# Modulation weights stored by output column and reduced along rows, with the first stage cut into nine groups

## The reference, cut to what matters

```python
c_act = jax.nn.silu(c)                                   # (1, 2048)
mod = c_act @ w_ada[l] + b_ada[l]                        # (2048, 12288): 100 MB
sh_a, sc_a, gt_a, sh_f, sc_f, gt_f = split(mod, 6)
h = _rmsnorm(x, norm_mix[l]) * (1.0 + sc_a) + sh_a
p = h @ w_in[l]                                          # (2048, 9296)
... attention (c_q, c_kv, k_pe) and gated delta rule (q, k, v, z, b, a) from p ...
mix = (g_a * y_a + g_b * y_b) @ w_o[l]
x = x + gt_a * mix
h = _rmsnorm(x, norm_ffn[l]) * (1.0 + sc_f) + sh_f
gate, up = split(h @ w_gate_up[l], 2)
x = x + gt_f * ((silu(gate) * up) @ w_down[l])
... final norm, then the second block: a_w_in_2, w_s, a_w_out_2 ...
```

## Time and profile before

| | us |
|---|---|
| median of 3 runs | 2282.92 (2281.2 to 2283.67) |
| the profiled execution | 2283.3 |
| its span | 2282.0 |
| TensorE busy in it | 2227.7 (98%) |
| VectorE | 1514.7 (66%) |
| ScalarE | 1017.8 (45%) |
| DMA, mean rate | 223 GB/s, 507.8 MB |

### The profile page before, as it was taken

How to read it: one execution, slowest core, us unless ns; L and a number is a source line. 1 busy time by engine, 2 the same in 40 slices (tenths; PEclk the granted TensorE clock), 3 DMA queues, 4 the chain that set the end, 5 groups by cost and what they waited for, 6 DMA issues and landing times.

```text
span 2282.0 us, 27023 instructions
## 1 busy us (share of the span) xinstructions
PE 2227.7 (98%) x10779; PEld 1856.2 (81%) x10779; DVE 1514.7 (66%) x1943; ACT 1017.8 (45%) x1287; POOL 24.5 (1%) x28
## 2 busy tenths in 40 slices
PE   5998999999999999999999999999999999999998
PEld 3778998888887888888888888887888888888886
DVE  5888998877759767765544555466556565655556
ACT  4345455333444464443344434456444444434444
POOL 0000000000000000000000000000000000000000
PEclk9999999999999999999999999999999999999999
DMA  9966868685778768865565565555565555555553
GB/s 361 381 242 203 276 222 276 197 281 185 238 283 292 282 233 285 275 236 197 188 198 185 185 203 185 190 197 194 187 201 189 189 189 189 189 186 195 198 189 132
DMA packets 278573, 507.81 MB, mean 223 GB/s; under 512 B 24104, under 2 KB 40240, under 8 KB 277424
## 3 DMA queue, kind: packets, MB, share of 16 engines
q1 hardware_dynamic: 278448, 506.09, 65.7%
HBM read 503.56 MB, written 2.50 MB: 222 GB/s over the span
## 4 chain that ended last, share of the span: by engine, by line
PE 81%; DVE 8%; DMA 4%; ACT 2%; issue 2%; SPq 1%; POOL 0%; DVEq 0%; ACTq 0%
PE bank L1212 24%; PE bank L1214 24%; PE bank L1213 24%; DVE WL L1954 3%; DMA RAW<-in_w_o_dram 2%; PE bank L1407 2%; ACT WH L1496 1%; DVE GA L1935 1%; PE bank L1133 1%; PE bank L1224 1%; PE bank L1226 1%; PE bank L1225 1%; DMA RAW<-in_w_in_dram 1%; DMA RAW<-in_w_o_gdn_dram 1%; PE bank L1160 1%
## 5 line engine op out<-in xcount | busy, mean ns | idle before, releaser
L1954 DVE TENSOR_TENSOR WL<-RAW,WH 128x1024 fp32r<-128x1024 f32 (+1 forms) x714 | 864.4, 1218 | 598.7 <-ACT WH L1496 596.9
L1496 ACT CAST WH<-RAW 128x1024 fp32r<-128x1024 f32 (+1 forms) x714 | 743.0, 1047 | 894.2 <-PE bank L1214 707.7
L1212 PE MATMUL bank<-WH,HTh 128*128 128x512 f32 x1936 | 766.0, 396 | 8.5 <-DVE WL L1954 8.0
L1214 PE MATMUL bank<-WH,HTl 128*128 128x512 f32 x1936 | 755.3, 390 | 0.0
L1213 PE MATMUL bank<-WL,HTh 128*128 128x512 f32 x1936 | 754.8, 390 | 0.0
L1212 PEld LDWEIGHTS bank<-WH,HTh 128*128 128x128 f32 x1936 | 364.3, 188 | 88.7 <-DVE WL L1954 13.2
L1214 PEld LDWEIGHTS bank<-WH,HTl 128*128 128x128 f32 x1936 | 364.0, 188 | 76.8
L1213 PEld LDWEIGHTS bank<-WL,HTh 128*128 128x128 f32 x1936 | 364.5, 188 | 74.8 <-issue 1.9
L1935 DVE SCALAR_TENSOR_TENSOR GA<-RAW,ST,GA 128x512 f32<-128x512 f32 x264 | 181.1, 745 | 12.4 <-DMA RAW<-in_w_ada_dram 7.7
L1212 PE MATMUL bank<-WH,R2h 128*128 128x512 f32 x408 | 162.0, 397 | 3.6 <-DVE WL L1954 3.6
L1213 PE MATMUL bank<-WL,R2h 128*128 128x512 f32 x408 | 159.9, 392 | 0.0
(11 more groups left out here) (280 smaller groups left out, 1773.0 us busy)
## 6 DMA issues: line engine op xcount, KB each, us to landing
RAW<-in_a_w_in_dram SPq DMA_DIRECT2D x96, 1024.0 KB, 5.1
RAW<-in_w_gate_up_dram SPq DMA_DIRECT2D x88, 1024.0 KB, 5.1
RAW<-in_w_ada_dram SPq DMA_DIRECT2D x80, 1024.0 KB, 5.3
RAW<-in_w_in_dram SPq DMA_DIRECT2D x63, 1024.0 KB, 5.0
RAW<-in_w_down_dram SPq DMA_DIRECT2D x44, 1024.0 KB, 5.0
RAW<-in_a_w_out_dram SPq DMA_DIRECT2D x32, 1024.0 KB, 5.0
A<-in_w_ada_dram SPq DMA_DIRECT2D x16, 1024.0 KB, 11.4
RAW<-in_w_o_dram SPq DMA_DIRECT2D x16, 1024.0 KB, 5.1
```

The lines of the kernel that those rows point to most:

```text
L1212: e.matmul(o, ah[:, s], hi[:, k, :], start=first, stop=False)
L1214: i = e.matmul(o, al[:, s], hi[:, k, :], start=False, stop=last)
L1496: e.copy(hi, rv).then_inc(S["hi"], 1)
L1954: e.tensor_tensor(lo, rv, hi.bitcast(F32), ALU.subtract).then_inc(S["lo"], 1)
```

## The change

- The host stores `w_ada` as 96 blocks of 1 MB, one for each 128 outputs, with the output on the partition and all 2048 inputs along the row (8 KB). One VectorE instruction multiplies a block by c, which lies on all partitions as a row (`CB`), sums along the row and starts from the bias: its accumulator is 128 outputs as a column. The later 64 blocks need nothing else.
- In the first 32 blocks VectorE takes 12 of 16 parts (1,536 columns). The host stores the last four parts with inputs on partitions, and TensorE multiplies them in four matmuls with one column, for which VectorE adds the result in (`cam`).
- c is spread to 128 partitions by four K=1 matmuls, tanh by ScalarE and a product by VectorE (`begin`).
- The first stage has nine groups of 2, 2, 2, 2, 2, 2, 2, 1 and 1 k tiles. Each loads its columns of `sc_a` and `sh_a`, and the halves of the group before come between them. The four jobs may use places 8 and 9. ScalarE makes the unrounded h too, x is squared and scaled by ScalarE and VectorE half each.
- Gate rows: the four columns of 128 outputs are stored to DRAM (512 words of 4 bytes) and loaded back as a row on all partitions, in eight pieces, where a matmul and a bias load were.
- Biases, gains, convolution weights and c come from the host as one table of columns; the constants are loaded in two parts, the second after the first stage.

```diff
+KF = 12
+GROUPS = [(2 * g, 2) for g in range(7)] + [(14, 1), (15, 1)]
+NG = len(GROUPS)
+LATER = [s + 4 * c + k for c in range(4) for s in (64, 48) for k in range(4)]
+LATER += [s + k for s in (32, 80) for k in range(16)]
+GATES = {"gta": 32, "gtf": 80}
...
     def plan_units(self, jobs, extra):
         u = self.units
-        u.extend(("g", ci, q) for ci in range(2) for q in range(4))
-        for c in range(4):
-            f = [("g", 2 * c + 2 + i // 4, i % 4) for i in range(8)] if c < 3 else []
-            w = [("w", j, 4 * c, 4) for j in jobs[:4]]
-            u.extend([w[0]] + f[:1] + [w[1]] + f[1:5] + [w[2]] + f[5:] + [w[3]])
+        sm, cq, ckv, conv = jobs[:4]
+        last = ()
+        for k0, n in GROUPS:
+            g = [("g", 16 + k0 + k) for k in range(n)] + [("g", k0 + k) for k in range(n)]
+            u.append(g[0])
+            if last:
+                u.append(("w", ckv) + last)
+            u.append(g[1])
+            if last:
+                u.append(("w", conv) + last)
+            u.extend(g[2:])
+            last = (k0, n)
+            u.extend([("w", sm) + last, ("w", cq) + last])
+        u.extend([("w", ckv) + last, ("w", conv) + last])
...
+        for gi, (_, n) in enumerate(GROUPS):
+            if gi:
+                self.front_half(sm, 2)
+                self.front_half(cq, 0)
+            else:
+                m = self.ms()
+                self.put("x_sq", m)
+            for k in range(2 * n):
+                self.ada(self.staged[0], self.units[self.staged[0]][1])
+                self.issue_loads()
+                if gi and k == 0:
+                    self.front_split(ckv)
+                elif gi and k == 1:
+                    self.front_half(ckv, 1)
+                    self.front_split(conv)
+                elif k == 0:
+                    self.put("x_sc", m)
+                elif k == 1:
                     self.put("xt")
+            if gi:
+                self.front_half(conv, 3)
+            self.put("cam", gi)
+            self.front_split(sm)
+            self.front_split(cq)
+            self.put("h", gi)
+        self.front_split(ckv)
+        self.front_split(conv)
+        self.put("load_cst2")
+        self.front_half(sm, 2)
+        self.front_half(cq, 0)
+        self.front_half(ckv, 1)
+        self.put("rope_tables")
+        self.front_half(conv, 3)
...
+    def gate_rows(self):
+        for name, j0 in GATES.items():
+            for c in range(4):
+                while ("mod", j0 // 4 + c) not in self.have:
+                    yield
+                yield
+                yield
+                self.put("gate_store", name, c)
+                for _ in range(3):
+                    yield
+                while (name, "free") not in self.have:
+                    yield
+                self.put("gate_load", name, c)
...
+            for t in range(KF, 16):
+                m = e.matmul(bank[5][:, at:at + 1], rv[:, t * P:t * P + P], L.cact[:, t - KF:t - KF + 1],
+                             start=t == KF, stop=t == 15)
...
         elif kind == "ada":
-            i, ci, q = args
-            rv = L.raw(sch.raw_slot(i), 4, 512)
+            i, col = args
+            w = KF * P if col < 32 else D
+            rv = L.raw(sch.raw_slot(i), 4, 512).rearrange("p t n -> p (t n)")[:, 0:w]
             W.wait_ge(f"raw{sch.raw_slot(i)}", sch.raw_value[i])
...
+            W.wait_ge("cact", 6)
+            e.tensor_tensor_reduce(out=rv, in0=rv, in1=L.CB[:, 0:w], scale=0.5, scalar=COL[:, col:col + 1], op0=ALU.mult,
+                                   op1=ALU.add, accum_out=L.MOD[:, col:col + 1]).then_inc(S["ga_dve"], 1)
...
+        elif kind == "gate_load":
+            name, c = args
+            n = c + 4 * (name == "gtf")
+            W.wait_ge("gt_out", 16 * n + 16)
+            W.wait_ge("gt_in", 16 * n)
             W.wait_ge("og_lo", 4)
...
+def modulation(w):
+
+    blocks = w.reshape(D, 96, P).transpose(1, 2, 0).copy()
+    tail = w[KF * P:].reshape(16 - KF, P, 96, P).transpose(2, 1, 0, 3)
+    blocks[0:32, :, KF * P:] = tail[0:32].reshape(32, P, D - KF * P)
+    return blocks
```

More of the change, by code:

```diff
@@ L393, in stage_next @@
         if u[0] == "g":
[L394 to L405, removed]
+            self.ada(i, u[1])
+            self.have |= {("mod", u[1] // 4)} if u[1] % 4 == 3 else set()
             self.issue_loads()
@@ L436, in fill, with ada @@
             self.stage_next()
[L438 to L442, removed]
-        yield
-        yield
-        q = 1 - self.current
-        while self.pending[q] in self.bg or (not 2 <= self.left <= min(5, self.total - 2) and not self.forced):
-            yield
-            q = 1 - self.current
-        self.put("mod", ci, q)
-        self.put("mod_e", ci, q)
-        self.ga_busy[ci % 2] = False
-        self.have.add(("mod", ci))
-        yield
+    def ada(self, i, col):
+        self.put("ada", i, col)
+        self.ga_n += 1
+        self.ga_of[col] = self.ga_n
+        read = (("mod_t", self.ga_n),) if col < 32 else ()
+        self.marks[("raw_free", self.raw_slot(i))] = (("ga_dve", self.ga_n),) + read
+        self.staged[0] += 1
@@ new lines, in front, with front_split @@
+        self.front_split(ckv)
[6 more added lines that the diff above has]
+        self.front_half(conv, 3)
+        self.have |= {("ht", kt) for kt in range(16)}
+    def front_split(self, j):
+        i = self.staged[0]
+        _, uj, t0, nkt = self.units[i]
+        assert uj is j
+        hid = len(self.halves)
+        place = self.free_place(j)
+        self.place.append(place)
+        self.after.append(self.user[place] + 1)
+        self.user[place] = hid
+        self.halves.append((j, t0, nkt, i, 0, nkt))
+        self.put("split", hid)
+        self.marks[("raw_free", self.raw_slot(i))] = (("lo", hid + 1),)
@@ L520, in front_unit, with front_half @@
         self.staged[0] += 1
         self.issue_loads()
-    def front_halves(self, j, where):
-        for _ in range(2):
-            self.put("half", self.used, where)
-            self.used += 1
+    def front_half(self, j, where):
+        assert self.halves[self.used][0] is j
+        self.put("half", self.used, where)
+        self.used += 1
         j.end = self.used
@@ L757, in mod_scale @@
         for q in range(4):
-            while ("mod", ci0 + 2 * q) not in self.have:
+            while ("mod", ci0 + q) not in self.have:
                 yield
@@ L1342, in pe_program @@
             held[n] = [("hl_lo", num)]
-        elif kind == "gt":
-            name, c, ci, n = args
-            W.wait_ge("ga_sum", ci - 7)
-            take(n)
-            e.matmul(bank[n], ones, L.GA[:, ci % 2, 0, :], start=True, stop=True).then_inc(S["mod_t"], 1)
-            held[n] = [("gt", ci - 15)]
         elif kind == "turn_t":
@@ L2748 @@
     host = {"x": np.asarray(inputs["x"])[0], "cst": shape_constants()}
+    host["cols"] = columns(inputs)
+    host["w_ada"] = modulation(np.asarray(inputs["w_ada"])[0])
     for name in _LAYER:
```

387 lines of the change are left out of this document (132 added, 255 removed).

## The result

The changed kernel takes 2304.47 us (median of 4 runs, 2301.09 to 2308.97) against 2283.07 before: ratio 1.0096, 95% interval 1.0076 to 1.0116. It is slower by 21 us, and 53 us slower than I predicted. Its profiled execution took 2301.09 us, span 2299.6, which is 17.6 more than the span before.

A forecast was written before the change was run, and what follows sets the result against it. DMA bounds the first stage until about 142 us, TensorE nearly all the rest. 2283.3 - 14.1 (matmuls) - 19.4 (first stage) + 2 (clock) - 1 (VectorE) = 2250.8, taken as 2251 us; 8-in-10 range 2240 to 2270.

The forecast's parts named there:

- Part 4: Gate rows' eight stores and loads on SP's queue cost nothing, waits covered by three weight buffers; uncovered, 20 us in all.
- The sign that I had named: SP's waits for stored rows showing among TensorE's releasers would prove the prediction wrong.
- Part 2: VectorE's later columns: 27 us of its work saved, worth 1 us of time (nothing to 4); no split comes later.
- Part 3: First stage, groups paced by DMA: second w_in job's first matmul at 136 us, 19.4 earlier than 155.44.
- 2 for the clock: After the 3.7 us stop before the next stage, TensorE at 1.2 GHz: up to 4.4 us, taken as 2.
- the stop that I named: At each first-stage group's end, TensorE stops about 1.3 us: a 5.5 us chain against 3.8 us of remaining work.
- my own sum (17.3 + 5.5 + 3): First group: last columns land at 17.3 us, chain at its end 5.5, DMA running short 3.
- limit of about 358 GB/s: Rival rule for HBM reads: long rows gain nothing, a group takes 16.3 us, time about 2263; no chance given.
- Part 1: TensorE after the first stage: 16 later chunks lose their matmuls, 7.1 and 7.0 us, together 14.1 us gained.
- C: Rival: TensorE falls to 1.2 GHz in the first stage and stays, 7.5 us lost per group, 2311; chance 0.05.
- B: Rival: first stage gains nothing, nine groups' chains add 2.4 us to each of eight, 2268 to 2272; chance 0.2.
- D: Rival: gain lost later, SP waiting at gate rows or VectorE late with splits, 2275 to 2288; chance 0.06.

The follow-up runs named there:

- experiment 2: Changed kernel without the eight stores of gate columns, rows loaded from another input, so gates left out: 2290.97 us, ratio 1.0034.
- experiment 5: Changed kernel with the gate stores kept but nobody waiting for them, rows loaded from another input: 2312.86 us, ratio 1.0126.
- experiment 6: Changed kernel with turned gates alone: TensorE turns four gate columns to rows, stored as four pieces of 512 bytes: 2292.36 us, ratio 1.0045.
- Experiment 3: Changed kernel with the attention one slot earlier (one empty step fewer ahead of its background work): 2296.06 us, ratio 1.0054.
- experiment 9: Changed kernel with three repairs together (gate columns turned, attention one slot earlier, column table padded to 320 words): 2266.89 us, ratio 0.9927.
- Experiments 7: Changed kernel with the column table padded from 264 to 320 words, arena at a multiple of 128 bytes: 2302.21 us, ratio 1.0086.
- 8: Kernel before the change with only the column table 8 words longer, moving the arena by 32 bytes: 2290.09 us, ratio 1.0032.
- experiment 13: Gate-column transposes two steps later, on the changed kernel with three repairs and rope tables behind the third group: 2262.96 us, ratio 0.9912.

## Why the prediction was wrong

I predicted 2251 and measured 2304.5. The 53 us, step by step:

**Part 4, gate rows costed at nothing (13.5 us). This step failed.** I had written that three buffers of 1 MB cover SyncE's wait, and priced the loss of that cover at 2 to 3 us a store by the wait. The stores have no row in the trace before, and I bounded them as a wait and not as work for the DMA engines. They take 11.4 us each and halve what the weight loads get while they run (experiments 2, 5 and 6); most of the loss is at the four up to 785 us. The sign that I had named, waits for stored rows among TensorE's releasers, did not show: from 600 to 1020 us it waited for splits alone, 14.4 us where it was 3.9 before. The cover itself was read from a busy share of 0.57 to 0.77, a mean. The chain of waits of the kernel before, which I did not read in this stretch, starts at 709 us with lines like these:

```profile
709.30 5.08 DMA RAW<-in_w_o_dram
715.36 1.06 ACT WH L1496
716.78 0.76 DVE GA L1935
717.56 5.16 DMA RAW<-in_w_o_dram
722.74 1.06 ACT WH L1496
```

Over 700 to 820 us 36.8% of that chain are w_o loads. There was no cover to spend.

**Part 2, "no split comes later" (about 17 us). This step failed too.** The lengths of the instructions were right and the conclusion did not follow, because the change also moved the attention by one slot. Part 2 asked how long a unit is, not what it lies beside. The unit had been hiding ScalarE's exponentials and the cast behind them; without it VectorE waited 11.2 us for casts in 265 to 335 us, and TensorE 14.8 for attention and splits. Experiment 3 puts 17 us on it by 627 us (-17.5 for -0.5), and experiment 9 agrees: 25.5 us less than with turned gates alone, of which 6 to 7 are the place of the arena.

**A step that was missing (6.2 us): where the arena begins.** The diff shows the table growing from 256 to 264 words, and I passed over it. Experiments 7 and 8 show it in both directions.

**Part 3, the first stage (8 us).** The mechanism was right and its size was off: 9.5 gained, where I had 19.4 less 2 for the clock. The pace of a group was right, though its own terms did not give the stop that I named (5.5 less 3.8 us are 1.7, not 1.3; measured are 1.1 on the mean of six). The first half started at 31.4 us, where my own sum (17.3 + 5.5 + 3) gives 25.8. VectorE's timeline shows the end of that group's chain:

```profile
22.42 1.81 DVE L1877 CUSTOM_DVE_ANT_0 A<-A,CB,COL 128x1536 f32<-128x1536 f32 x1
24.16 0.08 DVE L1877 DVE_READ_ACCUMULATOR2_ANT MOD<- 128x1 f32 x1
27.97 0.16 DVE L1911 TENSOR_TENSOR MOD<-MOD,bank 128x4 f32<-128x4 f32 x1 [3.73 <-PE bank L1127]
```

The row of c is ready at 13 us as I had it. Then a sum of squares of x, four reductions and the transposes of x ahead of the last two columns follow one another, and the buffers come free so late that the DMA falls to 201 GB/s in 20 to 24 us and 170 in 36 to 40. That is 5.6 us beyond the 3 that I had added for it. Another 3 went before the halves ended (140.6 for 132), and 1.6 in the stop. The low clock fits the 2 us that I took: about 6.8 us at 0.50, in which TensorE was busy two thirds of the time.

The Trainium skill's limit of about 358 GB/s for reads from HBM ("DMA: Bandwidth & Descriptors", "Where 436 GB/s comes from"), a rival in the prediction, does not hold here either: the stage after the change moves 374 GB/s on the mean of 22 to 142 us, dips and all.

**Part 1, 14.1 us of matmuls (some 9 us missing).** They are gone from the list, but the time is not all gained. Seven lie before 627 us and were gained: with three repairs the lag goes from -8.1 to -16.3. The other seven are eight matmuls. Four begin from 694 to 779 us, where the chain goes through the w_o loads: with three repairs the lag rises by 5.0 us from 627 to 812, and in experiment 13 by 0.4, where 3.5 less was due. Four begin from 873 to 1009 us, where the chain is TensorE's: of their 3.5 us 3.1 arrive by 1019. The sentence "on an engine that is 99% busy" took the share of a long stretch for the path through it.

**The chances.** C did not happen: the mean clock of 22 to 142 us is 0.97. Half of the gain that B would have taken was lost, but not by B's mechanism: the groups kept their pace, and 5.6 us went in the first one. D was the case, at 0.06, with a price of 20 us for SyncE's waits alone (added to 2251 that is 2271, below the 2275 where I let D begin) and none for late splits. Stores and attention cost 13.5 and 17; D's chance should have been several times that, since it had two independent ways to come true, and I had read neither stretch in the trace.

## What to carry to other kernels

Before work is moved or removed in a tuned kernel, read the chain of waits in exactly that stretch: an engine that is busy all the time may still have only as much slack as the next load has, and a filler instruction may be what hides another engine's latency. A store of single words is not priced by its bytes, and its price falls on the loads beside it; a column across the partitions is better turned before it is stored. Where several losses stand in one kernel, a repair tried alone can show less than it is worth. When a table ahead of other buffers changes its length, look where they begin.

With three such points mended the change makes the kernel faster: 2266.89 us, and 2262.96 with the rope tables and the transposes moved as well (ratio 0.9912, 0.9895 to 0.9928).

## What the runs showed of the hardware that I had not expected

- A matmul of 128 x 512 in fp32 that streams an operand whose start is 32 or 64 bytes past a multiple of 128 comes every 0.233 us; at a multiple of 128 (two places tried) every 0.227. One step of 32 bytes makes a kernel of 2283 us 7.4 us slower. Offsets of 96 bytes were not tried, and why it is so stays open.
- A store of 512 single words from 128 partitions takes 11.4 us, and while it runs weight loads of 1 MB fall from some 320 to 350 GB/s to about 165, at a DMA share of 0.99 to 1.29. In the kernel the four stores up to 785 us, where loads were on the path, cost 12.4 us, and the four behind, where none was, 2.5.
